# Top-16 routing of a product-key layer: 64 candidate pairs per head in place of 256, and tree sums of the matches

## The reference: what is computed

```python
s_top, i_top = lax.top_k(s, PEER_TOPK)
cand = s_top[..., 0, :, None] + s_top[..., 1, None, :]
cand_idx = i_top[..., 0, :, None] * PEER_KEYS + i_top[..., 1, None, :]
best, sel = lax.top_k(cand.reshape(B, S, PEER_HEADS, PEER_TOPK * PEER_TOPK), PEER_TOPK)
idx = jnp.take_along_axis(cand_idx, sel, axis=-1)
g = jax.nn.softmax(best, axis=-1)
```

## Time and profile before

| | before |
|---|---|
| median of 3 runs | 4809.08 us |
| the profiled execution, whole time | 4815.44 us |
| its span | 4813.8 us |
| PE, DVE, ACT, POOL busy | 80%, 63%, 31%, 27% of the span |
| HBM read and written | 905.76 MB and 150.47 MB |
| `up_and_lists` up to the first gathered dot product | from 2260 to 2853 us of the span |

### The profile page before, as it was taken

The page is one execution under the profiler, slowest core; times in us unless marked ns, Lnnn a source line. Parts: engine busy times, 40 slices in busy tenths (PEclk is TensorE's granted clock), DMA queues, the critical chain, the costliest instruction groups (busy, mean ns, idle before and its releaser), DMA issues. The chain is left out here.

```text
span 4813.8 us, 51034 instructions
## 1 busy us (share of the span) xinstructions
PE 3831.6 (80%) x17580; PEld 2763.0 (57%) x17580; DVE 3026.1 (63%) x5900; ACT 1490.2 (31%) x2161; POOL 1293.2 (27%) x1080
## 2 busy tenths in 40 slices
PE   2999998699967888697555556758998898898996
PEld 1666665488755777586344445535555565565553
DVE  5566666312344232596999976777777767776665
ACT  3444444244432124211655551111112112121211
POOL 0000000000001000000000026867766766675442
PEclk9989998699986998798667778879999999999998
DMA  3000000288952337111133449999999999999996
GB/s 132 22 20 22 22 24 11 87 303 284 356 216 96 131 121 289 57 39 50 42 121 116 123 161 359 363 356 390 397 381 394 387 385 391 392 397 366 372 366 255
DMA packets 386986, 1058.67 MB, mean 220 GB/s; under 512 B 33776, under 2 KB 102768, under 8 KB 383600
## 3 DMA queue, kind: packets, MB, share of 16 engines
q0 software_dynamic: 153504, 567.35, 30.8%
q1 hardware_dynamic: 185568, 351.11, 21.1%
q10 hardware_dynamic: 47728, 137.91, 7.4%
HBM read 905.76 MB, written 150.47 MB: 219 GB/s over the span
## 5 line engine op out<-in xcount | busy, mean ns | idle before, releaser
L2197 POOL DMA_INDIRECT ex_v_rows<-peer_v_dram,expert_of x512 | 623.2, 1217 | 297.5 <-PE psum L2426 150.0
L2329 DVE TENSOR_TENSOR y<-y,psum 128x512 f32<-128x512 f32 x512 | 349.8, 683 | 392.5 <-PE psum L384 356.7
L382 PE MATMUL psum<-in_hi 128*128 128x512 f32 x1024 | 442.8, 432 | 97.6 <-DVE in_lo L1918 52.5
L2322 DVE CUSTOM_DVE_ANT_1 ex_u_rows<-ex_u_rows,y 128x1024 f32<-128x1024 f32 x352 | 430.3, 1223 | 73.2 <-DMA ex_u_rows<-u_rows_scratch,expert_at 54.7
L2189 POOL DMA_INDIRECT ex_u_rows<-u_rows_scratch,expert_at x352 | 400.7, 1138 | 271.8 <-DVE dots L2322 173.3
L382 PE MATMUL psum<-in_hi,v_hi 128*128 128x512 f32 x1024 | 438.2, 428 | 11.3 <-DVE v_lo L2366 11.1
L383 PE MATMUL psum<-in_lo,in_hi 128*128 128x512 f32 x1024 | 424.9, 415 | 0.0
L384 PE MATMUL psum<-in_hi,in_lo 128*128 128x512 f32 x1024 | 422.7, 413 | 0.0
L2426 PE MATMUL psum<-ex_v_rows,ex_spread 128*32 128x512 f32 x2048 | 298.1, 657 | 151.6 <-DMA ex_v_rows<-peer_v_dram,expert_of 150.0
L383 PE MATMUL psum<-in_lo,v_hi 128*128 128x512 f32 x1024 | 411.9, 402 | 0.0
L384 PE MATMUL psum<-in_hi,v_lo 128*128 128x512 f32 x1024 | 410.3, 401 | 0.0
(11 more groups left out here) (357 smaller groups left out, 8734.6 us busy)
## 6 DMA issues: line engine op xcount, KB each, us to landing
y<-peer_v_dram SPq DMA_DIRECT2D x128, 512.0 KB
front_r_in<-peer_uT_dram SPq DMA_DIRECT2D x96, 512.0 KB
u_rows_scratch<-front_r_out ACTq DMA_DIRECT2D x96, 512.0 KB, 5.1
sc_u_raw<-peer_uT_dram SPq DMA_DIRECT2D x64, 512.0 KB
route_scratch<-sc_stage SPq DMA_DIRECT2D x32, 1024.0 KB
g<-route_scratch SPq DMA_DIRECT2D x128, 256.0 KB
front_w_raw<-w_in_dram SPq DMA_DIRECT2D x32, 512.0 KB, 5.4
gates_ada<-w_adaT_dram POOLq DMA_DIRECT2D x16, 1024.0 KB
```

The source lines that it names most:

```text
L382: pe.matmul(out, w_hi, x_hi, start=start, stop=False)
L2197: pool.indirect_dma_start(v_rows[:, r * LANES + lane], None, every_v, bass.IndirectOffsetOnAxis(ap=expert_of[:, m // 32, t:t + 1], axis=0) ...
L2322: dve.tensor_tensor_reduce(out=halves(u_rows[:, r]), in0=halves(u_rows[:, r]), in1=rows, scale=1.0, scalar=0.0, op0=ALU.mult, op1=ALU.add, ...
L2329: dve.tensor_tensor(to, to, ps[:, n % 4], ALU.add).then_inc(added, 1)
```

## The change

`cand` has 64 entries per head, in four strips: rank 0 of the first side with ranks 0 to 15 of the second, ranks 1 to 3 with 0 to 7, ranks 4 to 7 with 0 to 3, and ranks 8 to 15 with 0. Both lists are sorted, so a pair of ranks (i, j), counted from 0, has at least (i + 1)(j + 1) - 1 pairs that are no smaller, and a pair outside of these strips isn't needed for the top 16. The searches run over 64 entries. The two ranks are worked out from the position in a strip by small instructions of 128 elements (part 5). The sum over 16 is made by four additions of halves (8, 4, 2, 1). The buffers of gathered rows in the ring lie in the new tiles, with the same number and size.

```diff
--- before.py
+++ after.py
@@ -1648,6 +1648,9 @@
 
         nc, a, ps = self.nc, self.a, self.psum
         SEL = HEADS * TOPK
+
+        STRIPS = ((0, 0, 1, 16), (16, 1, 4, 8), (40, 4, 8, 4), (56, 8, 16, 1))
+        PAIRS = 64
         GROUP, QUAD = 8, 4
         PIECES = 8
         GROUPS = P // GROUP
@@ -1690,8 +1693,13 @@
         u_hi = [h2_hi[:, 2 * r:2 * r + 2, HALF:T] for r in range(SPLITS)]
         u_lo = [h2_lo[:, 2 * r:2 * r + 2, HALF:T] for r in range(SPLITS)]
         with ExitStack() as c:
-            cand = self.sb(c, "sc_cand", [P, HEADS, TOPK, TOPK])
-            cand2 = self.sb(c, "sc_cand2", [P, HEADS, TOPK * TOPK])
+            cand2_of = self.sb(c, "sc_cand", [P, 2, HEADS, PAIRS])
+            cand, cand2 = cand2_of[:, 0], cand2_of[:, 1]
+            eq_flat = self.sb(c, "sc_eq", [P, SEL * TOPK], F16)
+            prod_flat = self.sb(c, "sc_prod", [P, SEL * TOPK], F16)
+            half_sum = self.sb(c, "sc_half_sum", [P, SEL * TOPK], F16)
+            spot = self.sb(c, "sc_spot", [P, 3, SEL])
+            side = self.sb(c, "sc_side", [P, 3, SEL])
             best = self.sb(c, "sc_best", [P, HEADS, TOPK])
             pos = self.sb(c, "sc_pos", [P, HEADS, TOPK], U32)
             pos_i = self.sb(c, "sc_pos_i", [P, 2, SEL], U32)
@@ -1713,8 +1721,8 @@
             gelu = self.sb(c, "sc_gelu_t", [P, 2, HALF])
 
             rows = [w[:].rearrange("k s g n -> k (s g n)").bitcast(F32) for w in (away, second)]
-            flat_cand = (cand[:].rearrange("p h a b -> p (h a b)"), cand2[:].rearrange("p h c -> p (h c)"))
-            u_rows = [flat_cand[r // 2][:, r % 2 * D:(r % 2 + 1) * D] for r in range(4)]
+            u_rows = [cand2_of[:].rearrange("p s h c -> p (s h c)")]
+            u_rows += [w[:].bitcast(F32) for w in (eq_flat, prod_flat, half_sum)]
             u_rows += [w[:].rearrange("k s g n -> k (s g n)").bitcast(F32) for w in (w_hi, w_lo)]
             with nc.Block() as block:
                 @block.sync
@@ -1794,16 +1802,14 @@
                         shape = [P, HEADS, TOPK, TOPK]
                         val = vals[:, b].rearrange("p (h s) k -> p h s k", s=2)
                         idx = idxs[:, b].rearrange("p (h s) k -> p h s k", s=2)
-                        cflat = [cand[:, h].rearrange("p a b -> p (a b)") for h in range(HEADS)]
+                        cflat = [cand[:, h] for h in range(HEADS)]
                         weight = picks[:, 2].rearrange("p (h k) -> p h k", k=TOPK)
 
-                        half = lambda w: w.bitcast(F16)[:, 0:SEL * TOPK]
-                        eq_flat = half(cand2[:].rearrange("p h c -> p (h c)"))
-                        prod_flat = half(cand[:].rearrange("p h k a -> p (h k a)"))
-                        eq = eq_flat.rearrange("p (k a) -> p k a", a=TOPK)
-                        eq4 = eq_flat.rearrange("p (h k a) -> p h k a", h=HEADS, a=TOPK)
-                        prod = prod_flat.rearrange("p (k a) -> p k a", a=TOPK)
-                        prod4 = prod_flat.rearrange("p (h k a) -> p h k a", h=HEADS, a=TOPK)
+                        eq = eq_flat[:].rearrange("p (k a) -> p k a", a=TOPK)
+                        eq4 = eq_flat[:].rearrange("p (h k a) -> p h k a", h=HEADS, a=TOPK)
+                        prod = prod_flat[:].rearrange("p (k a) -> p k a", a=TOPK)
+                        prod4 = prod_flat[:].rearrange("p (h k a) -> p h k a", h=HEADS, a=TOPK)
+                        sums = half_sum[:, 0:SEL * TOPK // 2].rearrange("p (k a) -> p k a", a=TOPK // 2)
 
                         def matches(side):
                             do(dve.tensor_tensor(eq, pos_h[:, side].unsqueeze(2).to_broadcast([P, SEL, TOPK]),
@@ -1812,10 +1818,21 @@
                         def picked(side):
                             do(dve.tensor_tensor(prod4, eq4, idx[:, :, side].unsqueeze(2).to_broadcast(shape), ALU.mult))
                             all_so_far()
-                            do(dve.tensor_reduce(picks[:, side], prod, AXX, ALU.add))
+                            do(dve.tensor_tensor(sums, prod[:, :, 0:8], prod[:, :, 8:16], ALU.add))
+                            all_so_far()
+                            do(dve.tensor_tensor(prod[:, :, 0:4], sums[:, :, 0:4], sums[:, :, 4:8], ALU.add))
+                            all_so_far()
+                            do(dve.tensor_tensor(sums[:, :, 0:2], prod[:, :, 0:2], prod[:, :, 2:4], ALU.add))
+                            all_so_far()
+                            do(dve.tensor_tensor(picks[:, side], half_sum[:, 0:SEL * TOPK // 2].rearrange("p (k a) -> p a k", a=TOPK // 2)[:, 0],
+                                                 half_sum[:, 0:SEL * TOPK // 2].rearrange("p (k a) -> p a k", a=TOPK // 2)[:, 1], ALU.add))
                         all_so_far()
                         if part == 0:
-                            do(dve.tensor_tensor(cand[:], val[:, :, 0].unsqueeze(3).to_broadcast(shape), val[:, :, 1].unsqueeze(2).to_broadcast(shape), ALU.add))
+                            for start, i0, i1, width in STRIPS:
+                                strip = [P, HEADS, i1 - i0, width]
+                                do(dve.tensor_tensor(cand[:, :, start:start + (i1 - i0) * width].rearrange("p h (a b) -> p h a b", b=width),
+                                                     val[:, :, 0, i0:i1].unsqueeze(3).to_broadcast(strip),
+                                                     val[:, :, 1, 0:width].unsqueeze(2).to_broadcast(strip), ALU.add))
                             all_so_far()
                             for h in range(HEADS):
                                 do(dve.max(best[:, h, 0:8], cflat[h]))
@@ -1838,10 +1855,31 @@
                                 do(dve.max_index(pos[:, h, 8:16], best[:, h, 8:16], cand2[:, h]))
                         elif part == 5:
                             pflat = pos[:].rearrange("p h k -> p (h k)")
-                            do(dve.tensor_single_scalar(pos_i[:, 0], pflat, 4, ALU.logical_shift_right))
-                            do(dve.tensor_single_scalar(pos_i[:, 1], pflat, 15, ALU.bitwise_and))
+                            do(dve.tensor_single_scalar(pos_i[:, 0], pflat, 3, ALU.logical_shift_right))
+                            do(dve.tensor_single_scalar(pos_i[:, 1], pflat, 2, ALU.logical_shift_right))
+                            do(dve.tensor_copy(spot[:, 2], pflat))
                             all_so_far()
-                            do(dve.tensor_copy(pos_h[:], pos_i[:]))
+                            do(dve.tensor_copy(spot[:, 0:2], pos_i[:]))
+                            all_so_far()
+
+                            do(dve.tensor_scalar(side[:, 0], spot[:, 0], -1.0, 0.0, ALU.add, ALU.max))
+                            do(dve.tensor_scalar(side[:, 2], spot[:, 2], -48.0, None, ALU.add))
+                            all_so_far()
+                            do(dve.scalar_tensor_tensor(side[:, 1], spot[:, 1], -6.0, side[:, 0], ALU.add, ALU.max))
+                            all_so_far()
+                            do(dve.tensor_tensor(spot[:, 0], side[:, 1], side[:, 2], ALU.max))
+                            all_so_far()
+                            do(dve.tensor_copy(pos_h[:, 0], spot[:, 0]))
+                            do(dve.tensor_scalar(side[:, 0], spot[:, 0], 8.0, 8.0, ALU.mult, ALU.add))
+                            do(dve.tensor_scalar(side[:, 1], spot[:, 0], 4.0, 24.0, ALU.mult, ALU.add))
+                            do(dve.tensor_scalar(side[:, 2], spot[:, 0], 48.0, None, ALU.add))
+                            all_so_far()
+                            do(dve.tensor_tensor(side[:, 0], side[:, 0], side[:, 1], ALU.min))
+                            do(dve.scalar_tensor_tensor(spot[:, 1], spot[:, 0], 16.0, side[:, 2], ALU.mult, ALU.min))
+                            all_so_far()
+                            do(dve.tensor_tensor(side[:, 2], side[:, 0], spot[:, 1], ALU.min))
+                            all_so_far()
+                            do(dve.tensor_tensor(pos_h[:, 1], spot[:, 2], side[:, 2], ALU.subtract))
                             all_so_far()
                             matches(0)
                         elif part == 6:
```

## The result

The changed kernel takes 4766.9 us (median of 4 runs, 4764.31 to 4769.75); the kernel before took 4813.35 us beside it (4 runs). The ratio is 0.9909, with a 95% interval from 0.9883 to 0.9935. The forecast was 4763. In a later comparison the changed kernel had 4771.9 us against 4813.9, ratio 0.9910 (0.9895 to 0.9926). The profiled execution took 4768.2 us, its span is 4766.6.

What follows compares the result with a forecast made beforehand. DVE was taken to bound the back halves and block 0's front half, DMA the later front halves. Terms 28.8 + 7.0 + 10.5 = 46.3 us off the profiled 4815.4, with medians 6.4 lower, gave 4763 us; range 4745 to 4785.

Steps and rivals of the forecast that it cites:

- The price per routing: DVE work saved in one routing of 128 tokens, all parts together: 7.2 us, from 3.1 to 8.5.
- Searches: Maxima and position searches in each routing over 64 columns instead of 256: gains of 3.2 and 4.8 us per routing.
- Sums of pairs: In each routing, one 2048-column addition becomes four short ones taking 0.92 us: gain 1.4 us.
- rival B: Short DVE instructions in the routings have a floor: 21 us less gain, 4784 us; chance 0.13.
- the tree: Four additions replacing the sum of 16 in each routing, 1.91 us: gain 0.38 us, twice per routing, 0.75 together.
- Back halves: Four back halves, bound by DVE, each shorten by the full 7.2 us: 28.8 us.
- Front half of block 0: PE waits there for DVE's picks; earlier picks end PE's chunks sooner: 7.0 us gained.
- Later front halves: Blocks 1 to 3, DMA-bound: only the stores' earlier start counts, 3.5 us three times, 10.5 us.
- The gathers: Gathers behind the stage: ring, count and order unchanged, so nothing gained.
- Rival A: Later front halves give nothing, since DMA engines or loads end them at the same time: 4773 us; chance 0.12.
- Rival C: ACT takes over as bound in the back halves, losing half their gain, 14 us: 4777 us; chance 0.09.
- rival D: PE's lower clock level is kept through the front halves: 46 us slower, 4855 us; chance 0.04.

## Why the prediction came out right, and what in it did not

**The price per routing** was 7.2 us and measured 6.9. Searches: 0.127 and 0.193 us forecast for 64 columns, 0.129 and 0.194 measured. Sums of pairs 0.92 against 0.93, ranks 3.7 against 3.74. The line through 256 and 128 columns holds at 64, and rival B's floor is out. The term that was mis-sized is the tree: 0.38 us forecast per side, 0.27 measured (3.19 us with the product where it was 3.46), and the run without it confirms this by 0.53 us per back half. The additions of 1024, 512 and 256 columns took 0.69, 0.43 and 0.41 as priced, the last 0.39 instead of 0.29. That last one reads one 16-bit number and hops: 0.389 - 0.155 = 0.234 us for 128 columns is 1.83 ns a column against 1.04. The third addition's 0.41 is the slow form's 0.42; whether it ran in the fast form and paid for its hops no run here separates. By the rule that I weighed there (the Trainium skill, Vector Engine (DVE) Microarchitecture Reference, section 5.2) such hops cost extra, and the trace agrees for the last addition. The rule's highest figure, 2.5 ns a column, which it gives for 32-bit words that step 24 words, was the base of my estimate of 0.48 us, and that is more than either addition took. The bounds of the single terms, as they stand in the prediction, add up to 1.5 and 8.0 us per routing and not to its 3.1 and 8.5; the measured 6.9 lies inside both.

**Back halves.** 28.8 us forecast, 27.6 measured. That they are DVE's is shown by the run with more work there, which paid all of it, and by DVE's busy time. This is the largest part of the gain.

**Front half of block 0.** 7.0 us forecast, 6.7 measured, and PE and DVE meet there with 0.88 us between them.

**Later front halves.** The mechanism was that only the start of the stores counts and the rest of the shorter routing vanishes. Both sides of it are shown: 6.6 us of added DVE work in each leave them as they are, and moving two `split_low` in the kernel before gives nearly the same gain in these stretches (7.2 us of 8.3) without a shorter routing. The start moved as forecast, 3.35, 3.34 and 3.74 us by SP's rows, and DVE's waits for ACT's tile copies rose as forecast, from 6.0, 5.9 and 7.1 us to 10.9, 9.7 and 10.2. Of the 10.5 us only 8.3 arrived: from that load to the next first comparison the half took 44.25 us before (2411.93 to 2456.18) and 45.36 after (2399.83 to 2445.19). The assumption that failed is that the queue behind the stores has a fixed length. A late second load is not what is missing here: it goes out 12.36, 12.31 and 12.06 us behind the last comparison, where it was 17.37 or 17.38 in the kernel before (2419.30 at block 1):

```profile
2419.30 0.94 SPq L1730 DMA_DIRECT2D sc_u_raw<-peer_uT_dram  x1
```

It moved forward by 5 us and the half by 2.2 to 3.4. What makes the rest of the queue longer stays open.

**The gathers.** "Nothing" was forecast, but the profiles differ by 10.3 us from the first dot product on, 5.3 of them in the stretch of the dot products. This is not shown to be the change. The stretch was 309.7 and 310.6 us in two kernels with the old routing and 305.2 in the third; 304.3, 306.9, 305.4, 305.2 and 302.1 in those with the new one; 303.1, 301.5, 298.6 and 295.4 us in those with more buffers. The ranges of old and new touch, the DMA share is 0.98 before and after, and the experts' stage behind it differs by up to 10 us between profiles with nothing changed in it. A small part may be real; the old side has only three samples.

**The sum.** 46.3 us were forecast, the spans differ by 47.2 and the medians by 46.45, but part of that agreement is luck: the stage itself gave 41.8 us up to the gathers, 4.5 less than forecast (1.2 in the back halves, 0.3 in the first front half, 2.2 in the later ones, 0.8 in front of the gathers), the stages ahead took 4.9 from it, and everything from the first dot product on gave 10.3. Rival A would have kept the front halves at 54.25 us, and they did not stay there. Rival C fell with the back halves themselves, where 27.6 of 28.8 us arrived, and with the run that added work there, rival D with the granted clock, 0.86 in a later front half against 0.84.

## What to carry to other kernels

Cut a stage at instructions that recur and ask of each stretch separately who ends it; here the same saving of 6.9 us was worth 6.9 in one half and 2.2 to 3.4 in the other. In a stretch that a DMA queue ends, look for what the queue's first entries wait for, and for the place of the last entry that the stretch needs. In those halves moving two short instructions was worth nearly as much as all the DVE work saved, though the whole time doesn't show it. Two more tile buffers and a seventh tile ahead, by which that last load no longer stands behind all the stores, were worth 40 to 50 us, about as much again as the whole change. Short searches and elementwise instructions can be priced from two lengths of the same operation, but an operand that hops after each 16-bit number needs its own row.

## What the runs showed of the hardware that I had not expected

A two-input addition of 128 columns whose 16-bit inputs lie 16 bytes apart takes 0.389 us, one of 128 adjacent 32-bit columns 0.292 us.

An earlier start did not pass through this queue one to one: 3.3 us of earlier stores gave 1.8, -0.1 and 1.7 us with a late second load, and 2.6, 2.1 and 2.5 us with an early one.
